# Gated delta rule: the gated product and the low halves on GpSimd, the high halves and the first convolution at other places

## The reference

```python
qkv, z, b, a = split(h @ w_in)
qkv = silu(causal_depthwise_conv(qkv, conv_w))       # 4 taps in time
q, k = l2norm(q) * 128 ** -0.5, l2norm(k)            # 8 heads of q and k, each serves 2 of the 16 v heads
beta, g = sigmoid(b), -exp(A_log) * softplus(a + dt_bias)
# chunks of tokens, each with
L = strict_lower((k * beta) @ k.T * decay)
T = inverse(eye + L)
v_new = T @ (v * beta) - (T @ (k * beta * exp(g))) @ state
o = (q * exp(g)) @ state + (q @ k.T * decay) @ v_new
state = state * exp(g_last) + k_dec.T @ v_new
# and at the end, per head
o = rmsnorm(o, norm_w) * silu(z)
y = o @ w_out
```

## Time and profile before

| | |
|---|---|
| median of 3 runs | 2736.5 us (2734.27 to 2737.23) |
| the profiled execution | 2736.56 us, its span 2734.8 us |
| mean granted clock of TensorE | 0.998 of full speed |
| busy over the span | PE 98%, DVE 65%, ACT 47%, POOL 33% |
| the GDN turns | about 1868 to 2391 us of the span |

### The profile page before, as it was taken

The page is one execution under the profiler, slowest core; times in us unless marked ns, Lnnn a source line. Parts: engine busy times, 40 slices in busy tenths (PEclk is TensorE's granted clock), DMA queues, the critical chain, the costliest instruction groups (busy, mean ns, idle before and its releaser), DMA issues.

```text
span 2734.8 us, 40987 instructions
## 1 busy us (share of the span) xinstructions
PE 2681.2 (98%) x15550; PEld 2223.8 (81%) x15550; DVE 1787.3 (65%) x2641; ACT 1274.7 (47%) x2008; POOL 899.6 (33%) x751
## 2 busy tenths in 40 slices
PE   8999999999999999999999999999999999899998
PEld 6998888789888898887788998877777777777777
DVE  7974336569753687635956887348777777676664
ACT  4542232445323453223554543345555555467775
POOL 5520013136431264403733545104422222122232
PEclk9999999999999999999999999999999999999999
DMA  5343332223553325533213256322222222122222
GB/s 144 87 123 93 96 82 78 82 80 101 170 159 94 96 85 157 175 96 85 78 31 90 83 145 181 106 70 71 78 70 70 70 70 63 44 78 65 66 62 70
DMA packets 484876, 255.94 MB, mean 94 GB/s; under 512 B 17843, under 2 KB 478422, under 8 KB 484710
## 3 DMA queue, kind: packets, MB, share of 16 engines
q1 hardware_dynamic: 484534, 253.40, 32.4%
q10 hardware_dynamic: 176, 0.27, 0.0%
HBM read 251.51 MB, written 2.13 MB: 93 GB/s over the span
## 4 chain that ended last, share of the span: by engine, by line
PE 89%; DVE 6%; ACT 2%; issue 1%; POOL 1%; DMA 0%; SPq 0%; DVEq 0%; ACTq 0%; POOLq 0%
PE bank L281 60%; PE bank L978 12%; PE bank L2495 1%; PE bank L2526 1%; PE bank L2528 1%; DVE w_lo L267 1%; PE bank L2527 1%; DVE dsa_work L2191 1%; PE bank L3435 1%; PE bank L3427 1%; DVE small L2185 1%; PE bank L2640 1%; PE bank L3460 1%; DVE gdn_blocks L3030 1%; PE bank L1569 1%
## 5 line engine op out<-in xcount | busy, mean ns | idle before, releaser
L267 DVE TENSOR_TENSOR w_lo<-w_raw,w_hi 128x1024 fp32r<-128x1024 f32 x365 | 463.1, 1271 | 463.2 <-ACT w_hi L261 443.8
L281 PE MATMUL bank<-x_hi,w_hi 128*128 128x512 f32 x1808 | 737.7, 408 | 6.0 <-DVE w_lo L267 4.2
L281 PE MATMUL bank<-x_lo,w_hi 128*128 128x512 f32 x1808 | 707.8, 391 | 0.6 <-DVE x_lo L623 0.6
L281 PE MATMUL bank<-x_hi,w_lo 128*128 128x512 f32 x1808 | 707.5, 391 | 0.0
L261 ACT ACTIVATE w_hi<-w_raw 128x1024 fp32r<-128x1024 f32 x349 | 366.9, 1056 | 489.7 <-PE bank L281 440.7
L281 PEld LDWEIGHTS bank<-x_hi,w_hi 128*128 128x128 f32 x1808 | 340.4, 188 | 88.1 <-issue 16.5
L281 PEld LDWEIGHTS bank<-x_hi,w_lo 128*128 128x128 f32 x1808 | 340.1, 188 | 74.3
L281 PEld LDWEIGHTS bank<-x_lo,w_hi 128*128 128x128 f32 x1808 | 341.1, 189 | 68.1 <-DVE x_lo L623 3.9
L468 POOL TENSOR_TENSOR sumsq<-sumsq,sq 128x512 f32<-128x512 f32 x56 | 90.3, 1613 | 711.8 <-ACT sq L456 711.2
L281 PE MATMUL bank<-h_hi,w_hi 128*128 128x512 f32 x768 | 300.3, 391 | 0.0
L281 PE MATMUL bank<-h_hi,w_lo 128*128 128x512 f32 x768 | 299.0, 389 | 0.0
(11 more groups left out here) (542 smaller groups left out, 5070.1 us busy)
## 6 DMA issues: line engine op xcount, KB each, us to landing
w_raw<-in_ffn_wi_dram SPq DMA_DIRECT2D x176, 512.0 KB, 3.8
w_raw<-in_ffn_wo_dram SPq DMA_DIRECT2D x64, 512.0 KB, 3.5
w_raw<-in_ada_w_dram SPq DMA_DIRECT2D x48, 512.0 KB, 4.8
w_raw<-in_a_w_in_dram SPq DMA_DIRECT2D x48, 512.0 KB, 4.0
w_raw<-in_b_w_in_dram SPq DMA_DIRECT2D x32, 512.0 KB, 4.0
w_raw<-in_ffn_wo_dram SPq DMA_DIRECT2D x32, 384.0 KB, 3.1
w_raw<-in_even_w_in_dram SPq DMA_DIRECT2D x16, 512.0 KB, 4.0
w_raw<-in_a_w_out_dram SPq DMA_DIRECT2D x16, 512.0 KB, 3.5
```

What stands on the lines that cost most here:

```text
L267: dve.tensor_tensor(w_lo[s][:], w_raw[raw_of(b) % RAW][:], w_hi[s][:].bitcast(F32), ALU.subtract).then_inc(w_lo_done, 1)
L281: mm = pe.matmul(out, lhs[:, w], rhs(kt), start=first and kk == 0 and m == 0, stop=last and kk == len(kts) - 1 and m == 2)
```

## The change

Four things move, all in the GDN turns:

- `gated` (two products) and `low` (two subtractions) go from DVE to GpSimd, behind `kdec` and ahead of `front`. Their semaphores go from `GdnOut.dve` to a new `GdnOut.pool`, and those who wait for them wait for that one.
- ACT makes the high parts behind its second tap (`conv(1)`) and ahead of `fa`, and no longer behind `conv(2)`.
- DVE adds the taps of q (`conv(0)`) behind `hb` and ahead of `f2b`, and no longer ahead of `ga`.
- DVE makes the low part of the weight block of the point "vc" right behind that of "PT", and no longer behind `f2b`.

```diff
         class GdnOut:
             act = Steps(sem("gdn_out_act"), ["ln", "rs_1", "half_0", "rs_0"] + both(["hi"]))
-            dve = Steps(sem("gdn_out_dve"), ["on_1", "on_0"] + both(["o", "lo"]))
+            dve = Steps(sem("gdn_out_dve"), ["on_1", "on_0"])
+            pool = Steps(sem("gdn_out_pool"), [f"o_{h}" for h in range(2)] + [f"lo_{h}" for h in range(2)])
...
@@ gdn_pe, out_tile; the same edit in gdn_act, squares
-                    pe.wait_ge(*GdnOut.dve.after("lo_1", p))
+                    pe.wait_ge(*GdnOut.pool.after("lo_1", p))
...
@@ gdn_act, high
-                    act.wait_ge(*GdnOut.dve.after(f"o_{h}", p))
+                    act.wait_ge(*GdnOut.pool.after(f"o_{h}", p))
...
@@ gdn_act, turn
                     conv(1, j + 1, i, at, odd)
+                if p is not None:
+                    high(p)
                 a, b = slice(0, P // 2), slice(P // 2, P)
                 pe("f")
...
                 if more:
                     silu(0, i, at, odd)
                     conv(2, j + 1, i, at, odd)
-                if p is not None:
-                    high(p)
                 splits("f2")
...
@@ gdn_dve, turn
-                if more:
-                    if p is not None:
-                        dve.wait_ge(*gdn_gate(at, i, 1)[3])
-                    conv(0, j + 1, i, at, odd)
-                if p is not None:
-                    gated(p, [gdn_gate(at, i, h)[3] for h in range(2)])
+                splits("vc")
                 pe("g")
                 for n, r, src in (("ga", a, second(0)), ("gb", b, second(1))):
                     dve.tensor_copy(G.m[r, :], src[r]).then_inc(*done(n))
                 for n, r, src in (("ha", a, second(0)), ("hb", b, second(1))):
                     tt(n, halves(G.V1[r, :]), halves(src[r]), eye(r), ALU.add)
+                if more:
+                    if p is not None:
+                        dve.wait_ge(*gdn_gate(at, i, 1)[3])
+                    conv(0, j + 1, i, at, odd)
                 pe("f2")
                 dve.tensor_copy(G.F2[b, :], first(1)[b]).then_inc(*done("f2b"))
-                splits("vc")
-                if p is not None:
-                    low(p)
                 pe("v")
...
@@ gdn_pool (both functions were in gdn_dve before, with dve in place of pool)
+            def gated(p, gates):
+                for h in range(2):
+                    pool.wait_ge(*GdnOut.dve.after(f"on_{h}", p))
+                    pool.wait_ge(*gates[h])
+                    pool.tensor_tensor(G.sq[h][:], G.sq[h][:], G.zs[h][:], ALU.mult).then_inc(*GdnOut.pool.done(f"o_{h}"))
+
+            def low(p):
+                for h in range(2):
+                    pool.wait_ge(*GdnOut.act.after(f"hi_{h}", p))
+                    pool.tensor_tensor(G.o_lo[h][:], G.sq[h][:], G.o_hi[h][:].bitcast(F32), ALU.subtract).then_inc(*GdnOut.pool.done(f"lo_{h}"))
...
@@ gdn_pool, turn
                     tt(f"kd_{h}", t3(G.kdec[h]), t3(G.k_tok), by_col(G.kd, j * 2 + h), ALU.mult)
+                if p is not None:
+                    gated(p, [gdn_gate(at, i, h)[3] for h in range(2)])
+                    low(p)
                 if at.kind != "last":
```

More of the change, by code:

```diff
@@ L2732, in squares @@
                 if p is not None:
-                    act.wait_ge(*GdnOut.dve.after("lo_1", p))
+                    act.wait_ge(*GdnOut.pool.after("lo_1", p))
                 for u in range(2):
@@ L3009, in normed @@
                     dve.tensor_tensor(G.sq[h][:], G.sq[h][:], G.W5[h][:], ALU.mult).then_inc(*GdnOut.dve.done(f"on_{h}"))
-            def gated(p, gates):
-                for h in range(2):
-                    dve.wait_ge(*GdnOut.dve.after(f"on_{h}", p))
-                    dve.wait_ge(*gates[h])
-                    dve.tensor_tensor(G.sq[h][:], G.sq[h][:], G.zs[h][:], ALU.mult).then_inc(*GdnOut.dve.done(f"o_{h}"))
-            def low(p):
-                for h in range(2):
-                    dve.wait_ge(*GdnOut.act.after(f"hi_{h}", p))
-                    dve.tensor_tensor(G.o_lo[h][:], G.sq[h][:], G.o_hi[h][:].bitcast(F32), ALU.subtract).then_inc(*GdnOut.dve.done(f"lo_{h}"))
             def turn(j, p, i, at):
```

## The result

The changed kernel takes 2761.9 us (median of 4 runs, 2760.79 to 2762.34), the kernel before beside it 2736.9 us (2734.27 to 2737.93): 1.0092 times as long, 95% interval 1.0075 to 1.0110. It is slower, as forecast, but the forecast was 2752 and its range ended at 2760. The profiled execution took 2761.97 us, 25.4 more than that of before. All of it lies in the GDN turns. I measure a turn from the start of the first product of y to the same in the next turn.

| turn | first y | 1 | 2 | 3 | 4 | 5 | 6 | last |
|---|---|---|---|---|---|---|---|---|
| before | 1895.57 | 59.76 | 68.68 | 68.70 | 68.79 | 68.81 | 68.70 | 65.14 |
| after | 1897.23 | 63.16 | 72.24 | 72.80 | 71.26 | 72.86 | 71.27 | 68.82 |
| more | 1.66 | 3.40 | 3.56 | 4.10 | 2.47 | 4.05 | 2.57 | 3.68 |

The account below looks back on a forecast made before the run. TensorE, busy 98%, was taken as the bound, so only its waits count. Middle turns 10.2, first turn 1.9, last turn 1.1 and clock 2.5 sum to +15.7 us on 2736.56: 2752.3, range 2741 to 2760.

Parts of the forecast that it names:

- Middle turn, DVE's order: Six middle turns: waits before f2 and y go, v starts later, gains and losses cancel; 0.0 us, within 0.2.
- GpSimd's two pairs in the loop: Solve's loop, middle turns: gated and low pairs hold VectorE up 1.3 us each; F 1.7 us later, 10.2 in six.
- The clock: TensorE's granted clock falls after the longer waits in the first and last turns; 2.5 us, bounds 0 and 13.6.
- First turn: First turn: the convolution ahead of L3096's copy makes v later; +1.9 us, bounds 1.5 and 2.3.
- Last turn: Last turn: loop hold-up costs 2.2 us, low halves no longer waited for gain 1.1; net +1.1.
- ScalarE, and GpSimd's own time: Earlier high halves fit ScalarE's wait for F, and GpSimd is idle for its four instructions; no cost.
- 1: Rival: only the gated pair meets the solve's loop, the low pair falls behind the transpose; +5.7 us, 2742; chance 0.13.
- 2: Rival: GpSimd gives way to VectorE in the loop, so only the orders count; +1.1 us, 2737.7; chance 0.08.
- 4: Rival: v does not wait for L3096's copy in the middle turns, so faster; -8.2 us, 2728; chance 0.08.
- Rival 3: The clock falls in most middle turns; +26.8 us, 2763; chance 0.11.

Follow-up runs that it names:

- off_loop: Changed kernel with GpSimd's four instructions held back until the solve's loop is over and ScalarE's high halves made later; 2745.0 us, 1.0033.
- filled: Changed kernel with nine spare TensorE products ahead of the wait for the transpose, from the second turn on; 2756.2 us, 1.0077.
- off_loop_late_conv: As off_loop, with VectorE's convolution of q behind f2b in the middle turns, ahead of the copies of g in the first; 2729.3 us, 0.9975.
- late_conv_loop: Changed kernel with only VectorE's convolution of q moved behind f2b in the middle turns; GpSimd stays in the solve's loop; 2747.5 us, 1.0038.
- one_input: Changed kernel with plain one-input copies in place of GpSimd's two multiplications and two subtractions; 2742.6 us, 1.0024.
- gated_alone: Changed kernel with the low halves back on VectorE behind f2b, only the gated products on GpSimd; 2746.7 us, 1.0037.
- pool_halves: Changed kernel with each of GpSimd's four instructions cut into two of 128x256; 2748.8 us, 1.0042.
- pool_move_alone: Changed kernel with VectorE's convolution of q and split of vc back where they were before the change; 2752.5 us, 1.0058.

## Why the prediction was wrong in size

The mechanism was right: GpSimd holds DVE up in the solve's loop, F comes late, f2's wait turns into one before v. Two terms of the sum were too small.

1. *Middle turn, DVE's order: 0.0, within 0.2.* `off_loop` shows +0.2. Right. Of the wait before f2 nothing is left, v waits 1.8 us, y none.
2. *GpSimd's two pairs in the loop: 2.7 a turn, 1.7 behind the slack.* Measured 0.62+0.70 for the gated pair (1.34 expected) and 1.13+0.82 for the low pair (1.34 expected): 3.27, and F about 2.3 late (3.27 less the slack of 0.93, for which I had 0.97). **This step was mis-sized**: the gated pair cost what I expected, but I carried the price of the early loop (0.67) to its end, where a pair of steps is shorter and less is done beside a GpSimd instruction, and nothing beside one that DVE's operation met at its start (1.13). With the +0.2 it makes 2.5 a turn, 15.0 in six, where the sum had 10.2: 4.8 missing.
3. *The clock: 2.5.* By `filled` and the turn lengths 6 to 8 us, so about 5 missing. **This is the step that failed**: I held waits of 1.7 and 1.6 us for harmless since 1.6 had been, and the middle turns got 2.2 and 1.8, with a fall in four of six. Even the right sizes would not have given the count, since the same wait brings one in some turns only. Of the two waits that I had priced, the one before F in the last turn brought a fall; the one of 2.49 us before v in the first turn did not (the granted clock over the 4 us from 1892 and over the next 4 is 1.00).
4. *First turn +1.9:* +1.66, with v's wait 2.49 for 0.85.
5. *Last turn +1.1 without the clock:* `filled`, which has no fall there, shows +1.0. The three and a bit that I let fall into the loop cost 2.2 there, as said.
6. *ScalarE, and GpSimd's own time: nothing.* Right: the evacuation of F follows F, and the four end at 2089.3, long before y at 2105.42, behind which the first output tile stands.

4.8+5.3-0.2-0.1 is 9.8; 2762.0 less 2752.3 is 9.7. Of the rivals, 1, 2 and 4 are out: both pairs met the loop, DVE did give way, and v waits. Rival 3 was nearest, 2763, but not for its reason alone: it had a fall of 1.7 in every middle turn on top of a loop of 1.7, and there were four (0.9 to 1.6 each) on top of one of 2.5.

## What to carry to other kernels

Before work is moved to GpSimd, look at what VectorE does at that time: a chain of short operations with two SBUF inputs paid 0.6 to 1.1 us here for each GpSimd instruction of 1.27, while operations that read a bank paid nothing (the copies of g keep their 0.69 us beside it in `off_loop`); so put GpSimd's work beside those, or cut it as short as the steps. Of two results that TensorE waits for in turn, nothing may stand between them on the engine that makes them: the same convolution cost 1.8 to 2.0 us a turn between them (`off_loop` and `off_loop_late_conv`, the changed kernel and `late_conv_loop`) and about 1.1 ahead of both, against its place behind them, where no wait is left. And a new wait of TensorE near 2 us is to be priced with the clock, by the chance of a fall and not by its length alone.

## What was not expected of the hardware

- A GpSimd cast of one input, 0.62 us by itself, took 1.4 beside a VectorE operation with two SBUF inputs that had begun first (one_input); the longer time stands in the busy time of GpSimd, not in its idle time.
- The hold-up falls faster than the length: beside a loop whose step pairs take 0.55 us, GpSimd instructions of 1.27 us cost 0.62 to 0.70 each, of 0.74 us 0.08 to 0.18, of 0.62 us 0.05. Where DVE's operation was just starting it was more: 1.13, 0.50 and 0.21 to 0.28.
- Full clock was lost in 0 to 3 of the six middle turns where v waited 1.8 us and F mostly under 0.5 (0 in gated_alone, 1 in filled, 2 in off_loop and in pool_halves, 3 in one_input), in 3 and 4 where F waited 2.2 and v did not (late_conv_loop, pool_move_alone), in 4 with both (after), and in none of the six kernels in which neither waited, though f2 waited 1.2 to 1.6 in before. The longest of these waits, 2.63 us before F in turn 1, brought a fall in after and none in late_conv_loop and pool_move_alone. These are counts of one execution each. A fall cost 1.5 to 1.6 us where nothing else had slack, and down to 0.5 where another engine was late anyway.
